# The second plane of each output tile: added by engines, or by an accumulating transfer of GpSimd's queue

## What is computed

```
y[tok] = sum over the token's two experts of gate weight * expert output
x = x + gate_ffn * RMSNorm(y)          # RMSNorm over the 1024 channels, times a gain
```

## Time and profile before

| | |
|---|---|
| median of three executions | 1735.85 us |
| the profiled execution, its device time | 1732.28 us |
| its span, first to last instruction | 1730.4 us |
| last stage, issue of the first load of `fy` to the end of the span | 1688.1 to 1730.4 us |
| VectorE busy in the span | 755.3 us (44%) |
| ScalarE busy | 630.0 us (36%) |
| TensorE busy | 1620.1 us (94%) |
| GpSimd busy | 130.0 us (8%) |

### The profile page before, as it was taken

The page is one execution under the profiler, slowest core; times in us unless marked ns, Lnnn a source line. Parts: engine busy times, 40 slices in busy tenths (PEclk is TensorE's granted clock), DMA queues, the critical chain, the costliest instruction groups (busy, mean ns, idle before and its releaser), DMA issues. The chain is left out here.

```text
span 1730.4 us, 27681 instructions
## 1 busy us (share of the span) xinstructions
PE 1620.1 (94%) x11350; PEld 1155.0 (67%) x11350; DVE 755.3 (44%) x1392; ACT 630.0 (36%) x1195; POOL 130.0 (8%) x219
## 2 busy tenths in 40 slices
PE   6999888999999999999999999969999999999984
PEld 3889767888888889999999989743333333333331
DVE  4524346888888764454455464751000000000006
ACT  4535435666655553343534353311111111111112
POOL 0000011111111000000000030000000000000001
PEclk9999989999999999999999999979999999999997
DMA  9463461111111285373447564379999999999977
GB/s 371 164 209 131 168 212 35 53 53 45 48 53 53 77 289 189 128 267 129 164 139 253 180 209 141 115 313 428 425 425 396 426 427 427 423 425 387 372 300 302
DMA packets 97156, 404.62 MB, mean 234 GB/s; under 512 B 12503, under 2 KB 40439, under 8 KB 84088
## 3 DMA queue, kind: packets, MB, share of 16 engines
q1 hardware_dynamic: 84768, 380.23, 57.6%
q0 software_dynamic: 7248, 17.71, 2.6%
q10 hardware_dynamic: 5016, 4.93, 1.0%
HBM read 365.29 MB, written 44.84 MB: 237 GB/s over the span
## 5 line engine op out<-in xcount | busy, mean ns | idle before, releaser
L1157 ACT ACTIVATE wup<-wraw 128x1024 fp32r<-128x1024 f32 x120 | 126.7, 1059 | 264.2 <-PE ps L1957 226.2
L1617 DVE TENSOR_TENSOR wlow<-wraw,wup 128x1024 fp32r<-128x1024 f32 x120 | 146.7, 1224 | 155.6 <-ACT wup L1157 155.3
L1957 PE MATMUL ps<-wg,xT 128*32 128x512 f32 (+2 forms) x1200 | 160.0, 595 | 5.2 <-DMA wg<-w_gate 4.0
L1957 PE MATMUL ps<-wd,aT 128*32 128x512 f32 (+2 forms) x1200 | 155.5, 593 | 9.3 <-DMA wd<-w_down 7.9
L1957 PE MATMUL ps<-wu,xT 128*32 128x512 f32 (+2 forms) x1200 | 155.6, 594 | 1.1 <-DMA wu<-w_up 1.0
L1957 PE MATMUL ps<-h_up,wup 128*128 128x384 f32 (+1 forms) x384 | 124.7, 325 | 3.5 <-DVE wlow L1617 3.5
L1957 PEld LDWEIGHTS ps<-wd,aT 128*32 128x32 f32 (+2 forms) x1200 | 48.5, 114 | 112.8 <-issue 111.1
L1957 PE MATMUL ps<-h_up,wlow 128*128 128x384 f32 (+1 forms) x384 | 123.6, 322 | 0.0
L1957 PE MATMUL ps<-h_low,wup 128*128 128x384 f32 (+1 forms) x384 | 123.6, 322 | 0.0
L1957 PEld LDWEIGHTS ps<-wg,xT 128*32 128x32 f32 (+2 forms) x1200 | 45.9, 114 | 100.1 <-issue 97.7
L1957 PEld LDWEIGHTS ps<-wu,xT 128*32 128x32 f32 (+2 forms) x1200 | 47.1, 114 | 93.9 <-issue 91.8
(11 more groups left out here) (393 smaller groups left out, 3340.9 us busy)
## 6 DMA issues: line engine op xcount, KB each, us to landing
wg<-w_gate SPq DMA_DIRECT2D x32, 2048.0 KB, 16.5
wu<-w_up SPq DMA_DIRECT2D x32, 2048.0 KB, 14.8
wd<-w_down SPq DMA_DIRECT2D x32, 2048.0 KB, 16.2
wraw<-w_ga SPq DMA_DIRECT2D x24, 512.0 KB, 3.6
wraw<-w_gr SPq DMA_DIRECT2D x24, 512.0 KB, 3.8
wraw<-w_at SPq DMA_DIRECT2D x24, 512.0 KB, 3.6
wraw<-w_lr SPq DMA_DIRECT2D x24, 512.0 KB, 3.5
wraw<-w_out SPq DMA_DIRECT2D x24, 512.0 KB, 3.6
```

The source lines that it names most:

```text
L1157: act.activation(wup[n % UP][:, :, :], wraw[n % RAW][:, :, :], ACT.Copy).then_inc(w_rounded, 1)
L1617: V.tensor_tensor(wlow[n % RAW][:, :, :], wraw[n % RAW][:, :, :], wup[n % UP][:, :, :].bitcast(F32), ALU.subtract).then_inc(w_split, 1)
L1957: return pe.matmul(out, lhsT, rhs, start=start, stop=stop, skip_group_check=True)
```

## The change

Each tile's first plane is loaded by SyncE's queue into slot 0, half the bytes of the former load. GpSimd's queue then issues, for each tile in order, one transfer that reads the second plane from `y_dram` and adds it onto slot 0 (`accum_op`). It waits for the landing of the tile's first plane and, from tile 4 on, for the landing of the accumulating transfer of tile t - 4. ScalarE waits for that transfer's semaphore. VectorE's plane sums, TensorE's matmuls of the last stage and GpSimd's residual adds are gone; VectorE makes all nine residual adds.

```diff
 (SyncE)
-                sp.dma_start(fy[0:n, t, :, :], y_dram[0:2 * PLANE, :].rearrange("(k r) n -> r k n", k=2)[t * P:t * P + n, :, :]
-                             ).then_inc(ld_rows[t % LF], 16)
+                sp.dma_start(fy[0:n, t, 0, :], y_dram[t * P:t * P + n, :]).then_inc(ld_rows[t % LF], 16)
...
-                if t in BY_POOL:
-                    sp.wait_ge(y_pooled, BY_POOL.index(t) + 1)
-                else:
-                    sp.wait_ge(y_added, t + 1 - len([b for b in BY_POOL if b < t]))
+                sp.wait_ge(y_added, t + 1)
 (GpSimd)
-            pool.wait_ge(ld_x1, 32)
-            for t in BY_POOL:
-                pool.wait_ge(ch_fin2, 2 * t + 2)
-                pool.tensor_tensor(fy[:, t, 1, :], fy[:, t, 0, :], x1f[:, t, :], ALU.add).then_inc(y_pooled, 1)
+            for t in range(TILES):
+                n = P if t < BLKS else NS
+                pool.wait_ge(ld_rows[t % LF], 16 * (t // LF + 2))
+                if t >= LF:
+                    pool.wait_ge(f_sum[t % LF], 16 * (t // LF))
+                pool.dma_start(fy[0:n, t, 0, :], y_dram[PLANE + t * P:PLANE + t * P + n, :], accum_op=ALU.add).then_inc(f_sum[t % LF], 16)
 (ScalarE)
-                if t in BY_PE:
-                    act.wait_ge(f_pe, BY_PE.index(t) + 1)
-                else:
-                    act.wait_ge(f_sum, BY_DVE.index(t) + 1)
-                act.activation(fjunk[0:n, :], row_sum(t), ACT.Square, accum_out=fst[0:n, t, 0:1]).then_inc(ch_fin, 1)
+                act.wait_ge(f_sum[t % LF], 16 * (t // LF + 1))
+                act.activation(fjunk[0:n, :], fy[0:n, t, 0, :], ACT.Square, accum_out=fst[0:n, t, 0:1]).then_inc(ch_fin, 1)
 (VectorE)
-            add_second(0)
...
-                if t + 1 in BY_DVE:
-                    add_second(t + 1)
...
-                if t in BY_PE:
-                    pe_bank = 2 * BY_PE.index(t) % 8
-                    V.scalar_tensor_tensor(fy[0:n, t, 0, :].rearrange("p (h n) -> p h n", h=2), ps[0:n, pe_bank:pe_bank + 2, :], fst[0:n, t, 1:2],
-                                           G2[0:n, :].rearrange("p (h n) -> p h n", h=2), ALU.mult, ALU.mult).then_inc(ch_fin2, 1)
-                else:
-                    V.scalar_tensor_tensor(fy[0:n, t, 0, :], fy[0:n, t, 0, :], fst[0:n, t, 1:2], G2[0:n, :],
-                                           ALU.mult, ALU.mult).then_inc(ch_fin2, 1)
+                V.scalar_tensor_tensor(fy[0:n, t, 0, :], fy[0:n, t, 0, :], fst[0:n, t, 1:2], G2[0:n, :],
+                                       ALU.mult, ALU.mult).then_inc(ch_fin2, 1)
...
-                if t not in BY_POOL:
-                    V.tensor_tensor(fy[0:n, t, 1, :], fy[0:n, t, 0, :], x1f[0:n, t, :], ALU.add).then_inc(y_added, 1)
+                V.tensor_tensor(fy[0:n, t, 1, :], fy[0:n, t, 0, :], x1f[0:n, t, :], ALU.add).then_inc(y_added, 1)
 (TensorE)
-            for i, t in enumerate(BY_PE):
-                pe.wait_ge(ld_rows[t % LF], 16 * (t // LF + 2))
...
-                for h in range(2):
-                    for a in range(2):
-                        ins = mm(ps[:, (2 * i + h) % 8, :], ident[:, :], fy[:, t, a, 512 * h:512 * h + 512], a == 0, a == 1)
-                ins.then_inc(f_pe, 1)
```

More of the change, by code:

```diff
@@ L53 @@
 LF = 4
-BY_PE = [1, 2, 4, 5, 7]
-BY_DVE = [0, 3, 6, 8]
-BY_POOL = [1, 3, 5]
 N_SMALL, N_LATE = 7, 4
@@ L489, in build @@
         idx_seen = sem("idx_seen")
-        f_sum, f_pe, f_sq = sem("f_sum"), sem("f_pe"), sem("f_sq")
-        y_added, y_pooled, st_out = sem("y_added"), sem("y_pooled"), sem("st_out")
+        f_sum, f_sq = [sem(f"f_sum{i}") for i in range(LF)], sem("f_sq")
+        y_added, st_out = sem("y_added"), sem("st_out")
         st_side, st_kws = sem("st_side"), sem("st_kws")
         block = ctx.enter_context(nc.Block())
-        def row_sum(t):
-            n = P if t < BLKS else NS
-            if t in BY_PE:
-                return ps[0:n, 2 * BY_PE.index(t) % 8:2 * BY_PE.index(t) % 8 + 2, :].rearrange("p h n -> p (h n)")
-            return fy[0:n, t, 0, :]
         def bc(ap, shape):
```

## The result

The changed kernel took 1742.61 us (median of 18 executions, 1739.78 to 1747.41), the kernel before 1736.31 us beside it (1730.45 to 1741.67). The ratio is 1.0038, 95% interval 1.0028 to 1.0048: 0.4% slower, within the 0.5% that the prediction took as no change, at 1.6 us from the 1741 us forecast.

The account below looks back on a forecast made before the run. The last stage goes from DMA, then VectorE, to being bound by accumulating transfers: eight tiles at 3.84 us plus start and tail end 4.5 us later, rounded to 5; 1732.3 + 5 = 1737.3, plus 3.6 for a median: 1741 us, range 1731 to 1761.

Parts of the forecast that it names:

- f = 2: Last stage: an accumulating transfer costs two units, fetching from SBUF taking as long as from memory; chance of about this 0.45.
- units: Time for all 16 DMA engines to move the 512 KB of one plane of one tile: 1.28 us at 410 GB/s.
- The upper end f = 4: Accumulating transfers cut into small pieces: +25 us, 1761 us; chance of clearly dearer or serialized, over +8.7 us, 0.43.
- Turns of one row, 1 + f units a tile: Last stage: engines alternate 4 KB rows of the two queues; a tile takes 3.84 us while SyncE's queue has work.
- The bound moves from VectorE to the transfers: Last stage: accumulating transfers at 3.84 us a tile exceed VectorE's 2.75 us and become the bound.
- The start: Last stage: first plane lands after 3.6 us, GpSimd's issue takes 1.0 us, first byte 0.5 us later, accumulation begins at 1693.3.
- the tail from tile 7's sum to the end: After tile 7's sum at 1725.5: ScalarE 1.6, VectorE 2.75 twice, last store 1.9, 0.4 to the end at 1734.9 us.
- the f = 1 case: Rival, last stage: fetch of the old value hidden, VectorE the bound, -4.3 us; chance 0.10, including that with VectorE held.
- the rounding from 4.5 to 5 us: Forecast lengthening of the last stage, rounded up because row-by-row turns and the 410 GB/s are somewhat rough.
- GpSimd's adds: Last stage: VectorE instructions ran long beside GpSimd's adds; removing them takes 2.5 us off VectorE's work.
- GpSimd's issue holding VectorE: Rival, last stage: 1.0 us issue per tile stops VectorE; swallowed at two units, about +5 us with hidden fetch (jointly 0.10).
- Serialized: Rival: accumulations run one at a time, about 5.9 us a tile, end 21 us later; chance 0.43 shared with clearly dearer.

Follow-up runs that it names:

- e2: Changed kernel with GpSimd's queue started only after all first planes landed and stores held until all sums landed; stage 50.4 us, one execution.
- e3: Changed kernel with only SyncE's stores held until all sums have landed; stage 47.6 us, ratio 1.0029 against the kernel before.
- e8: Changed kernel with SyncE's last-stage loads and stores each split into two transfers of 2 KB rows; stage 47.9 us, ratio 1.0032 against the kernel before.
- e1: Changed kernel with GpSimd's transfers not adding, so the second plane overwrites slot 0; stage 38.8 us, ratio 0.9986 against the kernel before.
- e9: Changed kernel with at most two first-plane loads in SyncE's queue; stage 47.5 us, one execution.
- e7: Kernel before with the residual adds of tiles 1, 3, 5 on VectorE instead of GpSimd; stage 42.4 us, ratio 0.9999.
- e5: Changed kernel with each accumulating transfer issued only after the one before landed; stage 65.3 us, one execution.
- e10: Kernel before with only tiles 6 and 8 accumulated by GpSimd's queue, tile 6 loaded and accumulated early; stage 40.5 us, ratio 0.9985.

## Why the prediction was right

**The price of the adding, f = 2.** Right, and the step on which all hangs. Argued from loads alone and stores alone filling the engines at the same rate, it measured 1.94 units alone (e2) and 1.93 by packets beside the other queue. The Trainium skill's 1.93 (Collectives: The Full Stack, on why reduce-scatter is slower) agrees. What is measured is the price. That it is a second read is the reason given for it, and no run here separates this from another cost of the same size; the profile counts the bytes once (4.33 MB). The upper end f = 4 did not come because these rows of 4 KB are not cut up, as the packet counts show.

**Turns of one row, 1 + f units a tile.** It was an assumption; 3.84 us forecast, 3.79 us measured, and e3 (3.8, then 2.5 us) and e8 (3.2 us with half rows) show the mechanism and not only the number, together with the starts of the single rows 476 ns apart. The Trainium skill, DMA: Bandwidth & Descriptors, in the section on queues, rings and completion order, says that each engine goes round the queues packet by packet; the equal packet counts agree. It reckons some 9 to 17 descriptors to a packet, where a turn was a single row here.

**The bound moves from VectorE to the transfers.** Right: VectorE needs 1.28 + 1.22 + 0.16 us a tile, as summed, and idles 1 us between tiles. GpSimd's issue is 0.86 us (1.0 forecast) and hidden. e1 shows the other side, with VectorE as the bound again.

**The start: mis-sized.** The prediction has the first plane landing after 3.6 us and the first row of the accumulation 1.5 us after its issue. They took 4.0 us and some 4.5 us; from the first row to the landing it was then 4.6 us instead of 3.84 + 1.5 = 5.3. In the walk the first sum stood 1693.3 + 3.84 + 1.5 - 1688.13 = 10.5 us after the first load; it came after 13.1. Spacing gave 0.3 us back, and the tail from tile 7's sum to the end took 9.2 us (9.4 forecast). The sum: 46.8 us forecast for the stage, 48.9 measured. What failed is the assumption that turns begin at once: GpSimd's rows start behind what SyncE's queue already holds (e2, e9). The prediction let three units of first planes go ahead of the first accumulated row; it was nearly five. The 1.5 us itself was about right with the other queue empty (1.5 to 2.0 us in e2). In e1 the first sum was late in the same way, 10.7 us after the first load where the f = 1 case had 9.3.

That the median came within 1.6 us of 1741 is in part luck. The sum was 2.1 us short, and the rounding from 4.5 to 5 us, for which no row spoke, covered 0.5 of it.

**GpSimd's adds.** The 2.5 us of lengthened instructions were read rightly as caused by them (e7), but taking them away could not shorten the new stage, since it isn't bound by VectorE.

**The rivals.** GpSimd's issue holding VectorE: not seen, no VectorE instruction is over 1.29 us. Serialized: priced at 5.9 us a tile and found at 6.0 (e5), but not what the change does.

## What to carry to other kernels

An accumulating transfer is not a free add: it costs the DMA engines about twice a plain one (1.94 times here). Used for all nine tiles it made the transfers the bound and lost. It can pay only where another engine is the bound. Before taking work from an engine, ask in which part of the stage that engine is the bound; here the same operation lengthened the stage by 6.6 us when used for all nine tiles, and for two late ones shortened it by 1.0 to 1.5 us in single profiles, with ratios not clear of 1. Two queues share by packets, here one row each: the one with longer rows, or dearer ones, gets the larger share of the engines' time.

## What the runs showed of the hardware

- An accumulating transfer of 512 KB (128 rows of 4 KB, float32, memory onto SBUF) takes 2.49 us of all 16 engines; a plain one 1.28 us. GpSimd takes 0.83 to 0.97 us to issue it and 0.53 to 0.57 us for the plain one of e1.
- GpSimd's first row moved at most 2 us after the issue with SyncE's queue empty, and over 4 us behind a backlog of nearly five first planes, though later the two queues took turns row by row (605 packets against 607 in 16 us).
- A GpSimd add with both inputs in SBUF stretched VectorE's instructions beside it that also have both inputs in SBUF, from 1.28 to 3.27 us and from 1.22 to 2.39 us in e10. The multiply that reads PSUM (L1958) stayed at 1.28 us beside such an add. No net gain of giving GpSimd three adds could be measured (e7).
